# First sigmoid signals by itself, four places for survivals, and 84 of chunk 1's 124 convolution taps left to the feed-forward of chunk 0

## The chip, the cores and the metric

One core of a Trainium2 chip runs the whole program in one launch. The metric is device time in microseconds (us) of that launch, the median of several runs. Engines are named as in the profile: PE (TensorE, its matmuls), PEld (its weight loads), DVE (VectorE), ACT (ScalarE), POOL (GpSimd), SP (SyncE, which here issues every DMA). All arithmetic is 32-bit; a product of two numbers is made in three matmuls, from a high and a low part of each (the low part is a DVE subtraction behind an ACT copy).

## The reference, cut to what matters

One layer over 2048 prompt frames and 64 frames of a running stream, model width 1024:

```
h = RMSNorm(x);  a, gate, q, k, v = split(h @ w_in)
u = a * sigmoid(gate)
c = causal depthwise convolution of u, 31 taps, 512 channels
c = silu(LayerNorm(c)) @ w_pw
o[t] = sum over s < t of beta[t,s] * prod_{s<j<t} (1 - beta[t,j]) * v[s],   beta = sigmoid(q.k / 8)
x = x + concat(c, o) @ w_out
x = x + relu(RMSNorm(x) @ w_ff1)^2 @ w_ff2
```

The product over j is a running product from the right along each row of scores. The kernel makes it from sigmoid(-z), the "survivals" (tile `stay`), by a scan on DVE, and multiplies the result into sigmoid(z) (tile `beta`) on POOL.

## The kernel before

**Chunks and stages.** The prompt is cut into four chunks of 512 frames; the running stream goes with chunk 3. Each engine has its own instruction list, written out in one fixed order, and engines wait for each other on counted semaphores. The stages, in order: `ag(0)` and `kvq(0)` (chunk 0's projection and most of its convolution), `front` (92 slots: chunk 0's convolution end and attention, beside chunk 1's projection), `out(0)` (output projection and second norm of chunk 0), `window(0)` (128 slots of chunk 0's feed-forward, beside them chunk 1's last taps, LayerNorm, pointwise product and attention), `out(1)`, `ag(2)`, `kvq(2)`, `window(1)` with chunk 2's attention, `out(2)`, the same for chunk 3 with `window(2)`, and `window(3)` alone. One slot of a feed-forward window is twelve matmuls of 512 columns; 16 slots make one of 8 rounds (four slabs of w_ff1, then four of w_ff2).

**The convolution.** 124 taps (4 blocks of 128 channels, 31 each); a tap is one DVE instruction (line 1603) of 512 columns. `LATE[c]` is how many of chunk c's taps are left to the window; there they go two to a slot from slot 0 (`late_taps`). For chunk 1 the other taps are spread over the front by a list of due counts (`front_taps`). LayerNorm begins in slot `ln0(c) = (LATE[c] + 1) // 2` when the taps are done, the pointwise product 12 slots later, attention five slots after that (`att_first`) and up to slot 116 (58 in the front); the steps of attention are dealt out evenly over the slots in between.

**Attention.** One piece is 128 queries by up to 512 keys of one head. A step issues for several pieces at once, on each engine:

- PE: scores of piece z (line 2161, two PSUM banks), transposes of piece z-3 (2169, two banks), values of piece z-5 (2192)
- ACT (`att_sigmoids`): sigmoid(-z) into one of three `stay` tiles (1406), then sigmoid(z) into one of four `beta` tiles (1407), one signal `s_sg` behind both; then the high part of the transposed piece z-3 (1418)
- DVE (`att_parts`): for piece z-1 the edge copy (1810, pieces off the diagonal) and the scan (1811), both waiting for `s_sg`; then the low part of piece z-4 (1821); a mask (1799) on pieces of the diagonal
- POOL: `beta * stay` for piece z-1 (1135), waiting for the scan

ACT may overwrite a `stay` tile when the product that read it is done (`s_a`) and when the scan after it, which takes its first column over, is done (`s_scan`). PE may overwrite a bank of transposes when DVE has made the low part of the piece before last (`t_lo`).

**DMA.** Weights go through a ring of 8 slabs. At its first use a slab is loaded as 512 KB (line 734), split into high part (ACT, 1189) and low part (DVE, 1563) and stored (741, 1024 KB); later uses load both parts (736). All slabs of w_out and the feed-forward are first used in `out(0)` and `window(0)`. SP issues loads, stores, the keys (848), values (853) and queries (857) of attention and the mixed results (921, 936) in one order, sorted by planned ticks.

**Keys.** A block of 512 keys of the next head replaces the same block of the present one as soon as its last piece has been scored; with c+1 blocks in chunk c, its first use comes 2c+1 pieces later.

Of the kernel before, what the change touches and what calls it, by code (L numbers as in the profile page):

```python
# [5 lines left out]
F32 = mybir.dt.float32  # L6
F32R = mybir.dt.float32r
ALU = mybir.AluOpType
ACT = mybir.ActivationFunctionType
AX = mybir.AxisListType  # L10

P = 128
# [10 lines left out]
BANK = 512  # L23
# [10 lines left out]
KIB = 1024  # L34
# [24 lines left out]
def attention():  # L59

    out, z, m, v, o, hp = {}, 0, 0, 0, 0, 0
    for c in range(NC):
        for kind in range(2 if c == NC - 1 else 1):
            seq = []
            for head in range(NH):
                for p in range(1 if kind else 2):
                    for s in range(0 if kind else c, -1, -1):
                        rows = [(0, DEC)] if kind else [(P * i, P) for i in (2 * p, 2 * p + 1)]
                        for t, (q0, r) in enumerate(rows):
                            diag = kind == 1 or s == c  # L70
                            n = PAST + DEC if kind else q0 + P if diag else BANK
                            ends = t == len(rows) - 1
                            final = s == 0 and ends
                            brought = final and (kind == 0 or head == NH - 1)
                            seq.append(Piece(z, kind, head, p, t, q0, r, s * BANK, n, diag, ends, brought, m, v, o, hp, final))
                            z += 1
                            m += diag
                            v += ends
                    o += kind == 0 or head == NH - 1
                    hp += 1  # L80
            out[c, kind] = seq
    return out


ATT = attention()
# [39 lines left out]
LN_STEPS = 12  # L125

EARLY = 11
LATE = [20, 43, 36, 28]
FRONT = 92

MIX_AT = (62, 66, 71, 75)
# [3 lines left out]
def ln0(c):  # L135

    return (LATE[c] + 1) // 2

# [38 lines left out]
def gated_out(m):  # L177

    return max(8 * m + 8, ln0(0))
# [126 lines left out]
def build(nc, x_prompt, x_sample, cache_k, cache_v, state_conv, g_mix, w_in, w_dw, b_dw, g_cn, b_cn, w_pw,  # L306
# [3 lines left out]
    with ctx:  # L310
        top = [(nc.sbuf_base + 127) // 128 * 128]

        def region(size):
            o = top[0]
            top[0] += (size + 127) // 128 * 128
            return o

        def place(name, shape, dt=F32, offset=None):
            n = 4
            for s in shape[1:]:  # L320
                n *= s
            return nc.alloc_sbuf_tensor_at(name, shape, dt, offset=region(n) if offset is None else offset)
# [9 lines left out]
        o_cv = region(CB * CVP * 4)  # L332
        o_h = region(32 * KIB)
        o_a = region(56 * KIB)
# [34 lines left out]
        for c in range(2):  # L369
            n = TMAX if c else CHUNK  # L370
# [60 lines left out]
        aT_hi = place("aT_hi", [P, 2, 4, 2 * P], F32R, o_a + 22 * KIB)  # L431
        aT_lo = place("aT_lo", [P, 2, 4, 2 * P], F32R, o_a + 30 * KIB)
        beta = [place(f"beta{i}", [P, BANK], F32, o_a + (38 + 2 * i) * KIB) for i in range(4)]
        stay = [place(f"stay{i}", [P, BANK + 8], F32, o_a + 46 * KIB + i * (BANK + 8) * 4) for i in range(3)]
        o_o = o_a + 46 * KIB + 3 * (BANK + 8) * 4
        osb = place("osb", [P, 2 * P], F32, o_o)
        ohl = [place(f"ohl{i}", [P, 2, 2 * P], F32R, o) for i, o in enumerate((o_o + KIB, o_cv + 6 * KIB))]
# [22 lines left out]
        def sem(name):  # L460
            return ctx.enter_context(nc.semaphore(name))
# [29 lines left out]
        v_in = [sem(f"v_in{i}") for i in range(4)]  # L491
        q_in = [sem(f"q_in{i}") for i in range(3)]
        run_kq, run_v = sem("run_kq"), sem("run_v")
        z_ps, z_msk, s_sg, s_edge, s_scan, s_a, t_ps, t_hi, t_lo, v_ps, o_cp, o_sum, o_hi, o_lo = (
            sem(n) for n in ("z_ps", "z_msk", "s_sg", "s_edge", "s_scan", "s_a", "t_ps", "t_hi", "t_lo", "v_ps", "o_cp",
                             "o_sum", "o_hi", "o_lo"))
        o_st = [sem(f"o_st{i}") for i in range(2)]
        f1_ps, f_rel, f_sq, f_hi, f_lo, f2_ps, f2_add = (sem(n) for n in (
# [86 lines left out]
            return (before + e * (4 * len(splits(c)) + 2 * len(tiles(c))) + n) % 3  # L585

        Z_BANK, T_BANK, O_BANK = 3, 5, 7

        def ff_order(c):

# [42 lines left out]
        def front_taps():  # L633

            left, order, upto = [CW] * CB, [], []
            n, a = TAPS - LATE[1], gated_out(0)
            for t in range(FRONT):
# [13 lines left out]
        order_second, second_upto = front_taps()  # L651
        assert second_upto[-1] == TAPS - LATE[1]
        taps_in_order = [order_second if c == 1 else tap_order() for c in range(NC)]

        def taps_of(c, e):

            share = [3 if sec == "v" else 2 for sec, i, m in kvq_events(c)]
            rest, total = TAPS - 3 * EARLY - LATE[c], sum(share)
            return range(3 * EARLY + rest * sum(share[:e]) // total, 3 * EARLY + rest * sum(share[:e + 1]) // total)

        def late_taps(c, slot):
            return range(min(TAPS, TAPS - LATE[c] + 2 * slot), min(TAPS, TAPS - LATE[c] + 2 * slot + 2))

# [411 lines left out]
        def _(pool):  # L1075
# [51 lines left out]
            def att(c, step):  # L1127
                q = att_piece(c, step, 1)
                if q:
                    n = q.n - 1 if q.diag else q.n  # L1130
                    v = beta[q.z % 4]
                    pool.wait_ge(s_scan, q.z + 1)
                    if not q.diag:
                        pool.wait_ge(s_edge, q.z - q.m + 1)
                    nc.gpsimd.tensor_tensor(v[0:q.r, 0:n], v[0:q.r, 0:n], stay[q.z % 3][0:q.r, 1:n + 1],  # L1135
                                            ALU.mult).then_inc(s_a, 1)

            def window(c):
# [42 lines left out]
        def _(act):  # L1181
# [211 lines left out]
            def att_sigmoids(c, step):  # L1393
                q = att_piece(c, step, 0)
                if q is None:
                    return
                act.wait_ge(z_ps, q.z + 1)
                if q.diag:
                    act.wait_ge(z_msk, q.m + 1)
                if q.z >= 4:  # L1400
                    act.wait_ge(t_ps, q.z - 3)
                if q.z >= 3:
                    act.wait_ge(s_a, q.z - 2)
                    act.wait_ge(s_scan, q.z)
                z = ps[0:q.r, Z_BANK + q.z % 2, 0:q.n]
                nc.scalar.activation(stay[q.z % 3][0:q.r, 0:q.n], z, ACT.Sigmoid, scale=-1.0)  # L1406
                nc.scalar.activation(beta[q.z % 4][0:q.r, 0:q.n], z, ACT.Sigmoid).then_inc(s_sg, 1)  # L1407

            def att_later(c, step):
# [146 lines left out]
        def _(dve):  # L1556
# [244 lines left out]
            def att_parts(c, step):  # L1801
                q = att_piece(c, step, 1)
                if q:
                    v = stay[q.z % 3]
                    dve.wait_ge(s_sg, q.z + 1)
                    init = 1.0
                    if not q.diag:
                        dve.wait_ge(s_scan, q.z - 1)
                        init = stay[(q.z - 2) % 3][0:q.r, 0:1]
                        nc.vector.tensor_copy(v[0:q.r, q.n:q.n + 1], init).then_inc(s_edge, 1)  # L1810
                    nc.vector.tensor_tensor_scan(v[0:q.r, 0:q.n][:, ::-1], v[0:q.r, 0:q.n][:, ::-1],  # L1811
                                                 ones[0:q.r, 0:1].to_broadcast([q.r, q.n]), init,
                                                 ALU.mult, ALU.mult).then_inc(s_scan, 1)
                q = att_piece(c, step, TURN + 1)
                if q:
                    dve.wait_ge(t_hi, q.z + 1)
                    bank = ps[:, T_BANK + q.z % 2, :]
                    full = q.n // P
                    o = q.v % 2
                    if full:  # L1820
                        ins = nc.vector.tensor_tensor(aT_lo[:, o, 0:full, q.t * P:q.t * P + q.r],  # L1821
                                                      bank[:, 0:full * q.r].rearrange("p (a b) -> p a b", a=full),
                                                      aT_hi[:, o, 0:full, q.t * P:q.t * P + q.r].bitcast(F32), ALU.subtract)
                    if q.n % P:
                        w = q.n % P
                        ins = nc.vector.tensor_tensor(aT_lo[0:w, o, full, 0:q.r], bank[0:w, full * q.r:(full + 1) * q.r],
                                                      aT_hi[0:w, o, full, 0:q.r].bitcast(F32), ALU.subtract)
                    ins.then_inc(t_lo, 1)
                q = att_piece(c, step, VALUES + 2)
                if q and q.out:  # L1830
                    me = slice(0, P) if q.kind else slice(q.head % 2 * HD, q.head % 2 * HD + HD)
                    dve.wait_ge(o_hi, q.o + 1)
                    nc.vector.tensor_tensor(ohl[q.o % 2][me, 1, :], osb[me, :], ohl[q.o % 2][me, 0, :].bitcast(F32),
                                            ALU.subtract).then_inc(o_lo, 1)
                q = att_piece(c, step, VALUES + 1)
                if q and q.out:
                    dve.wait_ge(o_cp, q.o + 1)
                    for me, there, here in halves(q):
                        home = here(osb[me:me + HD, :])
                        ins = nc.vector.tensor_tensor(home, there(ps[me:me + HD, O_BANK, :]), home, ALU.add)  # L1840
                    ins.then_inc(o_sum, 1)
# [542 lines left out]
```

## Time and profile before

| | |
|---|---|
| median of 3 runs | 2859.02 us (2856.19 to 2863.88) |
| the profiled execution | 2860.11 us, span 2858.3 us |
| mean granted TensorE clock | 0.982 of full speed |
| PE busy | 2713.4 us, 95% of the span |
| DVE, ACT, POOL busy | 57%, 37%, 16% |
| DMA | 616 MB, mean 216 GB/s |

PE is busy nearly all the time from about 480 us on; its idle time lies mostly in the stages before (the front, out(0)) and in the attention of chunk 3. In time, `front` is about 170 to 410 us, `out(0)` 410 to 467, `window(0)` 467 to 911, the attention beside it 603 to about 880, `window(1)`'s attention about 1230 to 1550, `window(2)`'s 1940 to 2340.

### The profile page before, as it was taken

How to read it: one execution, taken by the hardware profiler on the slowest of the kernel's cores; microseconds unless marked ns; L12 is line 12 of the kernel's file. 1: busy time of each engine (PE TensorE's matmuls, PEld its weight loads, DVE VectorE, ACT ScalarE, POOL GpSimd, SP SyncE). 2: the span in 40 equal slices, each digit the busy share in tenths (PEclk: the TensorE clock that was granted, in tenths of full speed). 3: DMA queues.
4: the chain of work that ended last, by engine and by line, in shares of the span. 5: the costliest groups of instructions: out<-in, count | busy, mean ns of one | idle time of the engine just before them, and what ended most of it. 6: DMA issues, size and time to landing. Idle time of an engine off the chain costs nothing.

```text
span 2858.3 us, 37286 instructions
## 1 busy us (share of the span) xinstructions
PE 2713.4 (95%) x13872; PEld 2273.5 (80%) x13872; DVE 1640.4 (57%) x2653; ACT 1071.5 (37%) x2144; POOL 455.5 (16%) x460
## 2 busy tenths in 40 slices
PE   7878789999999999999999999999999999999999
PEld 6656577778888788778888797777788887898998
DVE  6887786757773468356665358636777742212122
ACT  4323533446562212345554112335666530221121
POOL 2212310012220011022221002102333310000000
PEclk9899899999999999999999999999999999999999
DMA  9596597777777658465554746844355457353442
GB/s 316 205 310 228 166 319 276 290 264 262 272 268 301 242 195 276 174 255 187 179 181 160 298 177 217 278 179 168 116 186 178 144 170 268 124 216 133 189 165 92
DMA packets 262046, 616.18 MB, mean 216 GB/s; under 512 B 23217, under 2 KB 159409, under 8 KB 213741
## 3 DMA queue, kind: packets, MB, share of 16 engines
q1 hardware_dynamic: 261869, 613.80, 60.0%
q8 instruction: 114, 1.87, 0.3%
q14 instruction: 63, 0.52, 0.0%
HBM read 444.79 MB, written 168.94 MB: 215 GB/s over the span
## 4 chain that ended last, share of the span: by engine, by line
PE 71%; DVE 14%; DMA 5%; ACT 4%; issue 4%; SPq 1%; POOL 1%; ACTq 0%; DVEq 0%; POOLq 0%
PE ps L1965 9%; PE ps L1967 9%; PE ps L1966 9%; PE ps L2221 7%; PE ps L2222 7%; PE ps L2223 7%; DVE stay L1811 4%; PE ps L2192 3%; PE ps L2169 3%; PE ps L2161 2%; DVE cacc L1603 2%; PE ps L2323 2%; PE ps L2324 2%; PE ps L2030 2%; PE ps L2325 2%
## 5 line engine op out<-in xcount | busy, mean ns | idle before, releaser
L1965 PE MATMUL ps<-h2T_hi,w_s 128*128 128x512 f32 (+1 forms) x1280 | 463.9, 362 | 7.6 <-DMA w_s<-w_scratch 3.4
L1135 POOL TENSOR_TENSOR beta<-beta,stay 128x512 f32<-128x512 f32 (+3 forms) x328 | 311.9, 951 | 918.9 <-DVE stay L1811 918.9
L1967 PE MATMUL ps<-h2T_hi,w_s 128*128 128x512 f32 (+1 forms) x1280 | 452.9, 354 | 0.0
L1966 PE MATMUL ps<-h2T_lo,w_s 128*128 128x512 f32 (+1 forms) x1280 | 452.5, 354 | 0.0
L1406 ACT ACTIVATE stay<-ps 128x512 f32<-128x512 f32 (+3 forms) x328 | 173.7, 529 | 427.0 <-DVE ps L1799 222.1
L1881 DVE TENSOR_TENSOR resid<-ps,resid 128x512 f32<-128x512 f32 x256 | 174.5, 687 | 246.3 <-PE ps L2223 245.9
L2221 PE MATMUL ps<-w_s,hid_hi 128*128 128x512 f32 x768 | 308.3, 401 | 0.0
L2223 PE MATMUL ps<-w_s,hid_hi 128*128 128x512 f32 x768 | 299.9, 390 | 0.0
L2222 PE MATMUL ps<-w_s,hid_lo 128*128 128x512 f32 x768 | 299.8, 390 | 0.0
L1481 ACT ACTIVATE ps<-ps 128x512 f32<-128x512 f32 (+1 forms) x160 | 81.8, 511 | 515.1 <-PE ps L1967 510.6
L1965 PEld LDWEIGHTS ps<-h2T_hi,w_s 128*128 128x128 f32 x1280 | 242.0, 189 | 39.1 <-DMA w_s<-w_scratch 3.6
L1967 PEld LDWEIGHTS ps<-h2T_hi,w_s 128*128 128x128 f32 x1280 | 241.8, 189 | 32.1
L1966 PEld LDWEIGHTS ps<-h2T_lo,w_s 128*128 128x128 f32 x1280 | 242.4, 189 | 27.9 <-issue 1.0
L1603 DVE SCALAR_TENSOR_TENSOR cacc<-uT,vecs,cacc 128x512 f32<-128x512 f32 (+1 forms) x360 | 259.8, 778 | 1.5
L1811 DVE TENSOR_TENSOR_SCAN stay<-stay,stay,ones 128x512 f32<-128x512 f32 x192 | 244.6, 1274 | 0.0
L1891 DVE TENSOR_TENSOR hid_lo<-ps,hid_hi 128x512 fp32r<-128x512 f32 x96 | 66.4, 691 | 259.4 <-ACT hid_hi L1491 259.4
L2169 PE MATMUL ps<-ident,beta 128*128 128x128 f32 (+1 forms) x1104 | 177.4, 276 | 28.6 <-DVE aT_lo L1821 27.8
L1821 DVE TENSOR_TENSOR aT_lo<-ps,aT_hi 128x512 fp32r<-128x512 f32 (+3 forms) x328 | 189.6, 578 | 14.9 <-ACT aT_hi L1418 9.7
L2161 PE MATMUL ps<-a_k,a_q 128*128 128x512 f32 (+3 forms) x640 | 183.4, 369 | 7.6 <-ACT beta L1407 4.5
L2169 PEld LDWEIGHTS ps<-ident,beta 128*128 128x128 f32 (+1 forms) x1104 | 132.9, 141 | 72.2 <-issue 47.4
L1418 ACT CAST aT_hi<-ps 128x512 fp32r<-128x512 f32 (+3 forms) x328 | 172.9, 527 | 21.3 <-PE ps L2169 16.8
L1407 ACT ACTIVATE beta<-ps 128x512 f32<-128x512 f32 (+3 forms) x328 | 172.1, 525 | 0.0
(211 smaller groups left out, 5212.2 us busy)
## 6 DMA issues: line engine op xcount, KB each, us to landing
w_s<-w_scratch SPq DMA_DIRECT2D x282, 1024.0 KB, 8.2
w_scratch<-w_s SPq DMA_DIRECT2D x94, 1024.0 KB, 8.7
w_raw<-in_w_ff SPq DMA_DIRECT2D x64, 512.0 KB, 5.5
a_k<-k_scratch SPq DMA_DIRECT2D x80, 256.0 KB, 3.8
a_v<-v_scratch SPq DMA_DIRECT2D x80, 256.0 KB, 3.9
a_q<-q_scratch SPq DMA_DIRECT2D x64, 256.0 KB, 4.5
w_raw<-in_w_in SPq DMA_DIRECT2D x20, 512.0 KB, 7.5
mix_scratch<-ohl SPq DMA_DIRECT2D x66, 128.0 KB, 3.0
```

The costliest lines, as they stand in the source:

```text
L1135: nc.gpsimd.tensor_tensor(v[0:q.r, 0:n], v[0:q.r, 0:n], stay[q.z % 3][0:q.r, 1:n + 1], ALU.mult).then_inc(s_a, 1)
L1603: nc.vector.scalar_tensor_tensor(out=acc, in0=uT[:, k, tap:tap + wd], scalar=vecs[:, k, tap:tap + 1], in1=acc, op0=ALU.mult, op1=ALU.add). ...
L1811: nc.vector.tensor_tensor_scan(v[0:q.r, 0:q.n][:, ::-1], v[0:q.r, 0:q.n][:, ::-1], ones[0:q.r, 0:1].to_broadcast([q.r, q.n]), init, ALU.mu ...
L1821: ins = nc.vector.tensor_tensor(aT_lo[:, o, 0:full, q.t * P:q.t * P + q.r], bank[:, 0:full * q.r].rearrange("p (a b) -> p a b", a=full), a ...
L1965: nc.tensor.matmul(out, w[0], x[0], start=start, stop=False)
L1966: nc.tensor.matmul(out, w[0], x[1], start=False, stop=False)
L1967: return nc.tensor.matmul(out, w[1], x[0], start=False, stop=stop)
L2161: ins = nc.tensor.matmul(ps[0:q.r, Z_BANK + q.z % 2, 0:q.n], x, a_k[:, k0:k0 + q.n], start=v == 0, stop=v == 1)
L2169: ins = nc.tensor.transpose(ps[0:w, T_BANK + q.z % 2, b * q.r:(b + 1) * q.r], beta[q.z % 4][0:q.r, b * P:b * P + w], ident[0:q.r, 0:q.r])
L2221: nc.tensor.matmul(o, hid_hi[x][:, k, q0:q0 + r], wh[:, c0:c0 + BANK], start=k == 0, stop=False)
L2222: nc.tensor.matmul(o, hid_lo[x][:, k, q0:q0 + r], wh[:, c0:c0 + BANK], start=False, stop=False)
L2223: ins = nc.tensor.matmul(o, hid_hi[x][:, k, q0:q0 + r], wl[:, c0:c0 + BANK], start=False, stop=k == 3)
```

## The change

Three edits. ACT's first sigmoid gets a semaphore `s_stay` of its own, and DVE's edge copy and scan wait for that in place of `s_sg`; POOL's product now waits for `s_sg` as well. From chunk 1 on (`OPENING` is the count of chunk 0's pieces, 32) there are four `stay` tiles instead of three, the fourth in the place of the convolution sums, and ACT's waits before the first sigmoid reach one piece further back. `LATE[1]` goes from 43 to 84: chunk 1's front takes 40 taps instead of 81, the late ones go on to slot 41 of window(0) instead of 21, `ln0(1)` moves from slot 22 to 42, the pointwise product from 34 to 54, the first attention step from 39 to 59; the last stays before slot 116.

```diff
-LATE = [20, 43, 36, 28]
+LATE = [20, 84, 36, 28]
...
-        stay = [place(f"stay{i}", [P, BANK + 8], F32, o_a + 46 * KIB + i * (BANK + 8) * 4) for i in range(3)]
+        stay = [place(f"stay{i}", [P, BANK + 8], F32, o) for i, o in enumerate(
+            [o_a + 46 * KIB + i * (BANK + 8) * 4 for i in range(3)] + [o_cv + 4032])]
...
+        OPENING = len(ATT[0, 0])
+
+        def stay_of(z):
+            return stay[z % 3] if z < OPENING else stay[z % 4]
...
                     v = beta[q.z % 4]
+                    pool.wait_ge(s_sg, q.z + 1)
                     pool.wait_ge(s_scan, q.z + 1)
...
-                    nc.gpsimd.tensor_tensor(v[0:q.r, 0:n], v[0:q.r, 0:n], stay[q.z % 3][0:q.r, 1:n + 1],
+                    nc.gpsimd.tensor_tensor(v[0:q.r, 0:n], v[0:q.r, 0:n], stay_of(q.z)[0:q.r, 1:n + 1],
                                             ALU.mult).then_inc(s_a, 1)
...
-                if q.z >= 3:
-                    act.wait_ge(s_a, q.z - 2)
-                    act.wait_ge(s_scan, q.z)
+                back = 3 if q.z < OPENING else 4
+                if q.z >= back:
+                    act.wait_ge(s_a, q.z - 2 if q.z < OPENING else max(q.z - 3, OPENING))
+                    act.wait_ge(s_scan, q.z + 3 - back)
                 z = ps[0:q.r, Z_BANK + q.z % 2, 0:q.n]
-                nc.scalar.activation(stay[q.z % 3][0:q.r, 0:q.n], z, ACT.Sigmoid, scale=-1.0)
+                nc.scalar.activation(stay_of(q.z)[0:q.r, 0:q.n], z, ACT.Sigmoid, scale=-1.0).then_inc(s_stay, 1)
                 nc.scalar.activation(beta[q.z % 4][0:q.r, 0:q.n], z, ACT.Sigmoid).then_inc(s_sg, 1)
...
-                    v = stay[q.z % 3]
-                    dve.wait_ge(s_sg, q.z + 1)
+                    v = stay_of(q.z)
+                    dve.wait_ge(s_stay, q.z + 1)
                     init = 1.0
                     if not q.diag:
                         dve.wait_ge(s_scan, q.z - 1)
-                        init = stay[(q.z - 2) % 3][0:q.r, 0:1]
+                        init = stay_of(q.z - 2)[0:q.r, 0:1]
```

## Rows read from the trace of the kernel before

**Rows 1.** The page: span, and busy time of each engine.

```profile
span 2858.3 us, 37286 instructions
...
PE 2713.4 (95%) x13872; PEld 2273.5 (80%) x13872; DVE 1640.4 (57%) x2653; ACT 1071.5 (37%) x2144; POOL 455.5 (16%) x460
```

**Rows 2.** Windows: stretch, length, busy per engine (PE, PEld, DVE, ACT, POOL), clock, DMA.

```profile
255.00:352.00 97.00, 72.67 (x364) 57.15 (x363) 68.79 (x140) 49.10 (x130) 32.80 (x35) 0.89 0.57 183
467.00:560.00 93.00, 91.21 (x378) 71.85 (x379) 69.26 (x96) 39.79 (x54) 2.69 (x3) 0.98 0.72 268
600.00:905.00 305.00, 302.19 (x1556) 254.57 (x1555) 211.71 (x327) 168.86 (x327) 58.99 (x64) 1.00 0.76 272
1230.00:1560.00 330.00, 328.74 (x1794) 279.33 (x1793) 224.43 (x375) 173.56 (x370) 92.97 (x94) 1.00 0.51 179
1935.00:2345.00 410.00, 392.04 (x2195) 327.40 (x2194) 294.84 (x512) 235.16 (x510) 133.11 (x136) 1.00 0.48 161
```

**Rows 3.** Waits of PE, 255 to 352 us: total us, times, longest.

```profile
PE ps L2169 <- DVE aT_lo L1821: 10.6, 13, 2.1
PE ps L2030 <- DVE raw_kq L1660: 9.0, 2, 5.1
```

**Rows 4.** Waits of DVE, the same stretch.

```profile
DVE stay L1811 <- ACT beta L1407: 19.8, 23, 1.2
```

**Rows 5.** Groups of ACT by line, the same stretch: busy us, mean ns.

```profile
L1407 ACT ACTIVATE beta<-ps 128x256 f32<-128x256 f32 (+3 forms) x31 | 13.6, 438 | 0.0
```

**Rows 6.** Instructions of line 1603, 365 to 422 and 467 to 532 us.

```profile
L1603 DVE SCALAR_TENSOR_TENSOR cacc_second<-uT,vecs,cacc_second x48: 742/745/752, 364.4 to 420.1; 128x512 f32<-128x512 f32 x48
...
L1603 DVE SCALAR_TENSOR_TENSOR cacc_second<-uT,vecs,cacc_second x42: 741/747/750, 467.0 to 531.5; 128x512 f32<-128x512 f32 x42
```

**Rows 7.** Waits of PE, 374 to 412 us.

```profile
PE ps L2042 <- DVE packed L1674: 4.4, 1, 4.4
```

**Rows 8.** Windows at the front's end, columns as in rows 2.

```profile
394.00:406.00 12.00, 8.87 (x26) 7.01 (x27) 10.27 (x17) 1.70 (x3) 2.87 (x2) 0.57 1.03 416
408.00:412.00 4.00, 2.56 (x15) 2.01 (x14) 3.62 (x7) 1.83 (x4) 2.06 (x1) 1.00 0.75 215
```

**Rows 9.** DMA queue, 374 to 452 us: packets, MB, share of 16 engines.

```profile
q1 hardware_dynamic: 20851, 26.97, 99.8%
```

**Rows 10.** Timeline of ACT and of PE, end of out(0).

```profile
451.88 1.06 ACT L1189 CAST w_s<-w_raw 128x1024 fp32r<-128x1024 f32 x1 [0.45 <-DMA w_raw<-in_w_ff]
...
467.18 0.79 PE L1965 MATMUL ps<-h2T_hi,w_s 128*128 128x512 f32 x1 [1.40 <-DVE h2T_lo L1588]
```

**Rows 11.** Line 848 (key loads), 600 to 900 us: who waited, landing.

```profile
  PE ps L2161: 2.5, 2
...
DMA to landing us min/median/max: 2.9/6.5/11.7
```

**Rows 12.** Instructions of line 2161 (scores), 600 to 900 us.

```profile
L2161 PE MATMUL ps<-a_k,a_q x128: 220/389/398, 602.9 to 857.2; 128*128 128x512 f32 x80, 128*128 128x128 f32 x16, 128*128 128x256 f32 x16, 128*128 128x384 f32 x16
```

**Rows 13.** Waits of PE, 1935 to 2345 us.

```profile
PE ps L2169 <- DVE aT_lo L1821: 15.8, 22, 1.2
```

**Rows 14.** Waits of DVE, 1935 to 2345 us.

```profile
DVE stay L1810 <- ACT beta L1407: 37.4, 64, 1.2
DVE stay L1811 <- ACT beta L1407: 27.2, 32, 1.2
```

**Rows 15.** Timeline of POOL and of DVE in chunk 3's attention.

```profile
2014.35 1.09 POOL L1135 TENSOR_TENSOR beta<-beta,stay 128x511 f32<-128x511 f32 x1 [2.34 <-DVE stay L1811]
...
2015.51 0.15 DVE L1810 COPY stay<-stay 128x1 f32<-128x1 f32 x1 [0.65 <-ACT beta L1407]
```

**Rows 16.** Timeline of DVE and of POOL in chunk 0's attention.

```profile
272.34 0.41 DVE L1833 TENSOR_TENSOR ohl<-osb,ohl 64x256 fp32r<-64x256 f32 x1
...
284.48 1.24 DVE L1833 TENSOR_TENSOR ohl<-osb,ohl 64x256 fp32r<-64x256 f32 x1
...
284.34 1.09 POOL L1135 TENSOR_TENSOR beta<-beta,stay 128x511 f32<-128x511 f32 x1 [1.34 <-DVE stay L1811]
```

More of the change, by code:

```diff
@@ L493, in build @@
         run_kq, run_v = sem("run_kq"), sem("run_v")
-        z_ps, z_msk, s_sg, s_edge, s_scan, s_a, t_ps, t_hi, t_lo, v_ps, o_cp, o_sum, o_hi, o_lo = (
-            sem(n) for n in ("z_ps", "z_msk", "s_sg", "s_edge", "s_scan", "s_a", "t_ps", "t_hi", "t_lo", "v_ps", "o_cp",
+        z_ps, z_msk, s_stay, s_sg, s_edge, s_scan, s_a, t_ps, t_hi, t_lo, v_ps, o_cp, o_sum, o_hi, o_lo = (
+            sem(n) for n in ("z_ps", "z_msk", "s_stay", "s_sg", "s_edge", "s_scan", "s_a", "t_ps", "t_hi", "t_lo", "v_ps", "o_cp",
                              "o_sum", "o_hi", "o_lo"))
```

## The prediction

> **What bounds the kernel now.** I read the page first, then a table of windows by stage, then PE's waits in the stages where it idles, then who makes those waits end, and last the DMA queue. PE is busy 2713.4 of 2858.3 us [rows 1], so whatever DVE, ACT or POOL save can return at most 145 us, and only where PE stands still. By stages [rows 2], it idles 24.3 us of 97 in chunk 0's attention, with a granted clock of 0.89, 1.8 of 93 beside the late taps of chunk 1, 2.8 of 305 in chunk 1's attention, 1.3 of 330 in chunk 2's and 18.0 of 410 in chunk 3's. The change can gain in the first and the last of these, and at the front's end, where PE stands before the transposes of line 2042 while DVE works through taps. It can lose in window(0), where PE hardly idles now.
>
> **Part 1: the first sigmoid's own signal.** In chunk 0's attention DVE stands 23 times, 19.8 us, for the second sigmoid [rows 4], though the scan reads only the first. The second is 438 ns on average [rows 5], so the scan can start that much sooner: 23 x 0.438 = 10.1 us from the chain of mask, sigmoid, scan, low part, mask. That is the upper end. The lower end is nothing, if the chain's other waits (a query load, the store of the mixed result, ACT's own copy behind the second sigmoid) end last. PE's two waits that hang on this chain are 10.6 and 9.0 us [rows 3], so there is room for all of it. I take half, 5 us.
>
> The added wait of POOL costs nothing: the scan, which POOL waits for anyway, starts behind the first sigmoid and lasts longer than the second. Behind POOL's waiting product stands only the next one. Should the scan ever end first, POOL would wait at most a second sigmoid's 0.44 us, for one piece.
>
> **Part 2: the four places, in chunk 3's attention.** PE's stall there is 15.8 us in 22 waits for the low part of line 1821 [rows 13]; DVE, which makes it, stands 64 + 32 times, 37.4 + 27.2 us, for the second sigmoid [rows 14]. With three places ACT can't begin piece z+1 before the scan of z has ended, so scan, two sigmoids and scan follow each other; with four and the early signal both sigmoids of z+1 lie beside the scan of z. Upper end: the whole 15.8 us and the 0.9 beside it.
>
> The lower end comes from POOL. In the steady pattern POOL's product begins at 2014.35 and lasts 1.09, to 2015.44; the edge copy before the next scan begins at 2015.51, having waited 0.65 us for the second sigmoid [rows 15]. A DVE instruction with two operands in SBUF seems to be unable to start beside such a product: line 1833 takes 0.41 us alone and 1.24 when it starts 0.14 us behind one, and it then ends 0.29 us behind the product's end [rows 16]. The scan too has two such operands. If it is held, it gains 0.07 us a piece off the diagonal and not 0.65, since the product is there until 2015.44. The 32 pieces of line 1811's own wait (the diagonal's, 27.2 us in all, 0.85 each) follow a mask and are further from the last product; they would keep their gain of up to 0.44 us, 14 us of chain in total. Also ACT no longer holds back the feed-forward's copy behind a first sigmoid that waits for a scan. Between all 16.7 and 5 (a third of the 14, as PE's stalls lie between the pieces that gain) I take 11 us: PE's stalls are 0.7 us each, about what a diagonal piece and the copy give back.
>
> The Trainium skill says this as a rule: "SBUF — State Buffer", section "SBUF: two separate sides", has DVE and GpSimd share one pair of ports under an exclusive lock, held for the whole instruction, also when the DVE instruction has two SBUF inputs; the other engine blocks fully. The trace agrees (1.24 against 0.41 us, rows 16). By that rule alone the early signal would be worth 0.07 us to each piece off the diagonal; it is weighed as the second rival below.
>
> In the attention of chunk 2 the same edit has 1.3 us of idle time to win; I count 1. It also shows that 105 steps in 81 slots, 1.3 a slot, need not make PE wait.
>
> **Part 3: 41 taps leave the front.** 48 taps of 745 ns run from 364 to 420 us [rows 6]; with 40 due instead of 81, the last 41 of them go, 30.5 us of DVE. For PE alone I count what stands around them: the wait of line 2042, 4.4 us [rows 7], the time lost at the lower clock behind it (8.87 us busy in 394 to 406 at a mean of 0.57 of 2.4 GHz, so largely at 1.2 GHz: 8.87 x 0.43 = 3.8), and 1.4 us idle at 408 to 412 [rows 8]: 9.6 us.
>
> But what comes next is a DMA. From 374 to 452 us the queue is 99.8% of 16 engines busy and moves 26.97 MB [rows 9], and SP issues in one order that the change leaves as it is. The last of the four feed-forward slabs makes ACT wait to 451.88, and DVE and ACT, in order, finish out(0)'s norm only behind these slabs; window(0) starts 15.3 us later, at 467.18 [rows 10]. So PE may reach the end of out(0) 9.6 us sooner and find the slabs no earlier. The gap that an earlier front closes in the queue is the 1 us in which its share is 0.75 [rows 8]; I allow as much again: 2 us. What part 1 gains comes ahead of this stretch and shifts it as a whole. Bounds: 0 and 9.6.
>
> **Part 4: the 41 taps in window(0), and what they push back.** They come at two a slot in slots 21 to 41. The stretch with such taps now has DVE busy 69 of 93 us and PE idle 1.8 [rows 2]; one more of the same costs 1 us, from 0 (all hidden behind twelve matmuls a slot) to 2. LayerNorm, pointwise product and their DMAs move 20 slots unchanged, into slots that look the same; the slabs of w_pw come one round later, before the same number of other slabs.
>
> Attention then has 57 slots for its 73 steps instead of 77. Work per PE is the same. What is shorter is the time in which keys must land: the next head's block is loaded three pieces before it is needed. 64 pieces are scored from 602.9 to 857.2 [rows 12], 4.04 us apart: three are 12.1 us. A bare slot is some 2.9 us (378 matmuls in 91.2 us [rows 2], times twelve), so the 77 slots' 77 x 4.04 x 73/77 = 295 us become 295 - 20 x 2.9 = 237 us, 3.25 us a step, 9.7 for three. Landing takes 2.9 to 11.7 us, median 6.5, SP's own delay comes on top, and two of 14 loads already make PE wait, 2.5 us [rows 11]. 2.4 us less for each: those two and perhaps a third wait longer or for the first time, 5 us. Bounds: 0 and 14 x 2.4 = 34. DVE's and ACT's load there rises from 212 and 169 of 305 us [rows 2] by a fifth to a quarter and stays under PE's.
>
> **Sum.** The profiled execution took 2860.1 us around a span of 2858.3: 2860.1 - 5 - 11 - 1 - 2 + 1 + 5 = 2847.1. It lies 1.1 above the median of the runs, 2859.0, so 2846 is forecast for the median, 0.45% faster.
>
> **Rivals.** *The DMA is not what ends out(0).* The queue's share counts packets that overlap; in 394 to 406 it moves 416 GB/s [rows 8], and at that rate 26.97 MB take 65 us, not 78. Then the 9.6 us of part 3 stand in full: 7.6 more, 2838. Against it: ACT waits for the last slab [rows 10]. The Trainium skill's "DMA: Bandwidth & Descriptors", section "Specifications", gives 435 GB/s as the fabric's ceiling, which by itself leaves that room; no run here shows the mean of 346 of this stretch rising.
>
> *POOL's product holds the scan*, so window(2) gives 3 us instead of 11, or the DMA eats the front's chain as well: 2854, within 0.3%. For it: rows 15 and 16. Against: stalls of 0.7 us are small beside 0.85 on the diagonal.
>
> *Slower: keys land late.* If each of the 14 loads of chunk 1's attention is as late as the shorter time makes it, 34 us instead of 5, the sum is 2860.1 + 15 = 2875, 2874 for the median. It decides from where the waits of line 2161 for `a_k` exceed 27 us in all. Against it: half of the loads land within 6.5 us [rows 11].
>
> **How the numbers follow.** 0.3% of the time, 8.6 us, is about what a measurement here can tell from no change. Forecast as summed 0.45 (2842 to 2851), no DMA bound 0.17, scan held or front lost 0.26, late keys 0.08, the other 0.04 on both sides. Faster by over 0.3% (under 2850.4): most of the forecast's case, all of the first rival, little of the second, 0.62; within: 0.29; slower: 0.09. The range must take in both the first and the second rival and an error of some 8 us beyond: 2830 to 2862.
>
> **What would show it.** Right: in chunk 0's and chunk 3's attention the waits of lines 1811 and 1810 for line 1407 are gone, and the wait of 2169 for 1821 in window(2) falls from 15.8 to about 5; no tap of chunk 1 after about 371 us, line 2042's wait gone, out(0) starting some 15 us sooner but window(0) only 7, with PE idle in front of line 1985 or 1965; `a_k` waits of some 7 us in window(0). The forecast is wrong if window(0) starts more than 12 us sooner, if scans in window(2) now start right at the end of POOL's products and PE's stall stays over 10, or if PE's waits in window(0) pass 20 us.

## The result: slower by 0.4%, the loss in one window

| | before | after |
|---|---|---|
| median of ten runs | 2860.4 us (2856.19 to 2863.88) | 2872.5 us (2865.57 to 2873.98) |
| ratio | | 1.0039, 95% interval 1.003 to 1.0049 |
| span of the profiled execution | 2858.3 us | 2870.4 us |

The change made the kernel slower by 12 us. 2846 was forecast, with a range up to 2862, so the result lies outside it and on the other side.

The stage boundaries, read in the timeline of PE (the first matmul of each stage), cut the 12.1 us of the two spans into four parts:

| stretch | before | after | change | forecast |
|---|---|---|---|---|
| start to window(0) | 467.2 | 467.5 | +0.3 | -7 |
| window(0), to out(1) | 453.1 | 478.6 | +25.5 | +6 |
| out(1) to window(2) | 876.7 | 877.1 | +0.4 | -1 |
| window(2) to the end | 1061.3 | 1047.2 | -14.1 | -11 |

Window(0) counts here to the first matmul of out(1): that is at 920.3 us in the kernel before, and its own last matmul starts at 919.0, not at about 911 as the section on the time before has it.

### The profile page after: what moved, and what is told of

Same layout as the page of the kernel before. It is cut to its first block and busy times, and to the rows that moved or that the text cites. A ratio compares the mean times of both kernels' runs of the same rounds, so it can differ in the third digit from the quotient of the medians.

```text
span 2870.4 us, 37421 instructions
## 1 busy us (share of the span) xinstructions
PE 2712.5 (94%) x13872; PEld 2274.2 (79%) x13872; DVE 1671.7 (58%) x2653; ACT 1069.2 (37%) x2144; POOL 449.2 (16%) x460
## 5 line engine op out<-in xcount | busy, mean ns | idle before, releaser
L1819 DVE TENSOR_TENSOR_SCAN stay<-stay,stay,ones 128x512 f32<-128x512 f32 x192 | 276.0, 1438 | 0.0
```

## The profile after

The page of the changed kernel, the span and the engines (lines are 7 or 8 higher than before in this kernel):

```profile
span 2870.4 us, 37421 instructions
...
PE 2712.5 (94%) x13872; PEld 2274.2 (79%) x13872; DVE 1671.7 (58%) x2653; ACT 1069.2 (37%) x2144; POOL 449.2 (16%) x460
```

PE does the same work in more time. DVE is busy 31 us longer with the same 2653 instructions, against [rows 1]: some of them now take longer; the run with a thin product below shows it for 20 us of them.

Windows over the stretches of [rows 2]: length, busy time of PE, PEld, DVE, ACT and POOL, clock, DMA.

```profile
255.00:352.00 97.00, 70.77 (x365) 56.57 (x363) 71.24 (x141) 48.27 (x128) 30.30 (x35) 0.91 0.58 185
467.00:560.00 93.00, 92.46 (x392) 75.14 (x393) 76.80 (x107) 29.19 (x40) 0.00 (x0) 0.97 0.67 255
600.00:905.00 305.00, 283.51 (x1434) 235.20 (x1434) 208.04 (x327) 163.44 (x320) 65.63 (x68) 0.98 0.68 235
...
1935.00:2345.00 410.00, 399.96 (x2249) 337.92 (x2248) 312.62 (x508) 234.19 (x507) 133.81 (x136) 1.00 0.48 159
```

The taps are hidden in 467 to 560 us, where PE idles 0.5 us. The loss is in the third row: in chunk 1's attention PE idles 21.5 us of 305 where it idled 2.8, and the clock is 0.98 in place of 1.00. As the stages have moved, here are the same columns for whole stretches, before and after: window(0), then window(2) up to out(3), with chunk 3's attention in it.

```profile
467.18:920.26 453.08, 446.36 (x2160) 368.94 (x2161) 299.98 (x447) 222.51 (x402) 62.46 (x68) 1.00 0.73 268
...
1797.00:2380.80 583.80, 560.41 (x2956) 463.49 (x2954) 365.65 (x633) 285.04 (x601) 143.97 (x145) 1.00 0.53 184
```

```profile
467.52:946.10 478.58, 456.10 (x2161) 373.14 (x2161) 326.89 (x488) 222.06 (x402) 65.63 (x68) 0.98 0.70 251
...
1823.20:2392.50 569.30, 557.00 (x2956) 464.29 (x2954) 384.06 (x633) 284.45 (x602) 144.74 (x145) 1.00 0.55 189
```

In window(0) PE idles 22.5 us in place of 6.7, and the same matmuls keep it busy 9.7 us longer, at a mean granted clock of 0.98 in place of 1.00: together the 25.5 us. The stretch with chunk 3's attention gained: 12.3 us idle in place of 23.4.

PE's waits in 600 to 905 us (total us, times, longest):

```profile
PE ps L2177 <- DVE aT_lo L1829: 8.7, 8, 2.5
PE ps L2169 <- DMA a_k<-k_scratch: 8.7, 3, 6.5
PE ps L2200 <- DMA a_v<-v_scratch: 1.6, 1, 1.6
```

Half of it is the late keys that the prediction looked for, with 8.7 us in place of some 7. The other half is the low part of the transposed product, of which it says nothing.

**What stands in front of the low part.** DVE's timeline ahead of one such wait, and PE's line that ends it:

```profile
754.23 4.63 DVE L1571 TENSOR_TENSOR w_s<-w_raw,w_s 128x1024 fp32r<-128x1024 f32 x4 [0.93 <-ACT w_s L1196]
758.77 0.95 DVE L1819 TENSOR_TENSOR_SCAN stay<-stay,ones 128x384 f32<-128x384 f32 x1
759.64 0.40 DVE L1829 TENSOR_TENSOR aT_lo<-ps,aT_hi 128x256 fp32r<-128x256 f32 x1
...
760.19 0.63 PE L2177 MATMUL ps<-ident,beta 128*128 128x128 f32 x4 [1.72 <-DVE aT_lo L1829]
```

Four new w_ff2 slabs of a round are due at once, and their low parts (the splitting of a weight at its first use) stand in DVE's list in one block of 4.63 us. The scan and the low part of attention come behind it, in order, and PE may not overwrite the bank before. DVE is far from full in this stretch (208 of 305 us); here it is the order of its list that makes PE wait.

**What stands in front of the keys.** SP's timeline, and the wait of PE that the key load ends:

```profile
765.00 3.35 SPq L747 DMA_DIRECT2D w_scratch<-w_s  x4
768.45 1.20 SPq L740 DMA_DIRECT2D w_raw<-in_w_ff  x1
769.70 3.67 SPq L854 DMA_DIRECT2D a_k<-k_scratch  x1
...
782.29 1.22 PE L2169 MATMUL ps<-a_k,a_q 128*128 128x512 f32 x2 [6.50 <-DMA a_k<-k_scratch]
```

The same four slabs are stored, 4 MB, ahead of a key load of 256 KB, with one slab load of 512 KB between them; the keys land 12.6 us after their issue. Around the 6.50 us gap, in 780 to 800 us, the mean granted clock is 0.83, between the two levels of 1.2 and 2.4 GHz; in the kernel before it is 1.00 in the same 20 us.

**The front.** out(0) started 9.2 us sooner (400.78 against 410.03) and ended 0.3 us later. ACT's timeline in out(0) (the first slab of w_out, and the four of the feed-forward that made it wait in [rows 10]), PE's wait near the start, and the start of window(0), which answers to the last line of [rows 10]:

```profile
414.01 1.04 ACT L1196 CAST w_s<-w_raw 128x1024 fp32r<-128x1024 f32 x1 [10.41 <-DMA w_raw<-in_w_out]
...
447.86 4.01 ACT L1196 CAST w_s<-w_raw 128x1024 fp32r<-128x1024 f32 x4
...
419.63 0.69 PE L2050 MATMUL ps<-ident,packed 128*128 128x128 f32 x2 [6.81 <-ACT kqT_late L1302]
...
467.52 0.79 PE L1973 MATMUL ps<-h2T_hi,w_s 128*128 128x512 f32 x1 [1.40 <-DVE h2T_lo L1596]
```

ACT now stands 10.41 us for slabs of w_out that have not landed, and PE 6.81 us behind a copy that comes after their split on ACT. The wait for taps turned into a wait for a transfer. For the feed-forward's slabs at 447.86 it no longer waits.

**Chunk 3's attention.** The waits of PE and of DVE there, against [rows 13, 14]:

```profile
PE ps L2177 <- DVE aT_lo L1829: 5.3, 11, 0.7
...
DVE stay L1819 <- ACT stay L1414: 17.2, 32, 0.7
...
DVE stay L1818 <- ACT stay L1414: 5.9, 7, 1.3
```

## The experiments

The times are medians of four to ten runs, with the kernel before run on the same chip; it stood at 2858.95 to 2860.87 us throughout. Lengths of stages are read as above; window(0) lasts 453.1 us before and 478.6 after, and from window(2) to the end it is 1061.3 and 1047.2 us.

### Which edit loses, which gains

**LATE alone.**

```diff
-LATE = [20, 43, 36, 28]
+LATE = [20, 84, 36, 28]
```

> The kernel before with LATE[1] = 84 alone, three places and the old signal. Theory A, crowding: window(0) loses its 25 us because chunk 1's attention has 57 slots in place of 77, whatever the signal does; then out(1) starts about 945 us, window(2) keeps the 15.8 us of waits for the low part that it had before, and the time is about 2872 + 14 = 2886 us. Theory B, the four places and the early signal themselves upset window(0), since ACT runs further ahead there: then out(1) starts about 920 us and the time is 2855 to 2862 us.

Measured: 2896.5 us, ratio 1.013 (1.0115 to 1.0146). Window(0) lasts 487.2 us, window(2) to the end 1061.3 as before. PE's waits in 600 to 905 us:

```profile
PE ps L2169 <- DVE aT_lo L1821: 18.2, 16, 2.6
PE ps L2161 <- DMA a_k<-k_scratch: 6.2, 3, 4.7
```

The time is 10 us above what theory A gave, and theory B falls. The loss is that of LATE, and without the other two edits it is 34 us: they save 8.6 us of it in window(0), where the wait for the low part is 18.2 us without them and 8.7 with them.

**Early signal and four places, LATE[1] = 43.**

```diff
-LATE = [20, 84, 36, 28]
+LATE = [20, 43, 36, 28]
```

> The changed kernel with LATE[1] back at 43: early signal and four places alone. Theory A, crowding: out(1) starts about 918 to 920 us as before, window(2) gives its 14 us, and the time is about 2846 us, faster than both kernels. Theory B, signal and places upset window(0): out(1) starts about 945 us and the time is about 2871 us.

Measured: 2844.2 us, ratio 0.9947 (0.9932 to 0.9962): faster than both kernels, by 16 and 28 us. Window(0) lasts 453.8 us.

**The attention squeezed, without the taps.** As the run before, and:

```diff
 def att_first(c):
-    return pw_slot(c) + pw_step(c) * CB + 1
+    return pw_slot(c) + pw_step(c) * CB + 1 + (20 if c == 1 else 0)
```

> LATE[1] = 43 with early signal and four places, but chunk 1's attention still begins in slot 59 of window(0): the 73 steps in 57 slots without the 41 taps there. Theory A, crowding: the loss comes back without the taps, out(1) about 945 us, 2868 to 2873 us. Theory C, the taps in slots 21 to 41 or what they delay are what costs: out(1) about 920 us, about 2846 us.

Measured: 2873.45 us, ratio 1.0046 (1.0031 to 1.006), window(0) 480.5 us. Theory C falls: the taps cost nothing in window(0), the later start of attention all of it.

**LATE[1] = 63.**

```diff
-LATE = [20, 84, 36, 28]
+LATE = [20, 63, 36, 28]
```

> The changed kernel with LATE[1] = 63: attention of chunk 1 in 67 slots of window(0), between 77 and 57. If the loss begins at once and is even, half of it is here, 12 to 14 us: about 2857 us. If the work on new slabs stays covered down to some density, under 6 us is lost: 2845 to 2850 us. In either case window(0) starts at 466 to 471 us, the front's taps being no bound.

Measured: 2870.7 us, ratio 1.004 (1.0025 to 1.0054), window(0) 481.6 us. Both expectations failed: with 67 slots the window is no shorter than with 57, so the number of slots isn't the measure. (Window(0) starts at 464.4 us, a little sooner than expected.) DVE's timeline ahead of PE's longest wait for a low part there, and that wait:

```profile
638.66 5.76 DVE L1571 TENSOR_TENSOR w_s<-w_raw,w_s 128x1024 fp32r<-128x1024 f32 x5
...
645.59 1.20 DVE L1571 TENSOR_TENSOR w_s<-w_raw,w_s 128x1024 fp32r<-128x1024 f32 x1
...
646.77 2.05 DVE L1819 TENSOR_TENSOR_SCAN stay<-stay,stay,ones 128x512 f32<-128x512 f32 x1
648.75 0.26 DVE L1829 TENSOR_TENSOR aT_lo<-ps,aT_hi 128x128 fp32r<-128x128 f32 x1
...
649.15 1.09 PE L2177 MATMUL ps<-ident,beta 128*128 128x128 f32 x4 [4.14 <-DVE aT_lo L1829]
```

Here five splits of slabs fall in one block ahead of a scan, a sixth behind it.

### Is it the work on new slabs?

**New slabs ready.** LATE[1] = 84; from round 2 of window(0) on no slab counts as new. They are read from the scratch, where another matrix lies.

```diff
-        if all((kind, j) != (k, i) for k, _, i in W[:n]):
+        if all((kind, j) != (k, i) for k, _, i in W[:n]) and not (kind in ("f1", "f2") and j >= 8):
...
-                    sp.dma_start(w_s[:, slot, :].bitcast(F32), w_d[W_ID[kind, j]]).then_inc(w_in_s[slot], 16)
+                    there = ("ag", j % 8) if kind in ("f1", "f2") and j >= 8 else (kind, j)
+                    sp.dma_start(w_s[:, slot, :].bitcast(F32), w_d[W_ID[there]]).then_inc(w_in_s[slot], 16)
```

> The changed kernel, LATE[1] = 84, without new feed-forward slabs from round 2 of window(0) on: these slabs are read as 1024 KB from places of the scratch that hold other weights, so no high or low part of them is made and none of them is stored (the feed-forward's weights are wrong for that). Theory A1, the work on new slabs (split on ACT and DVE, stores ahead of the keys) is what the denser attention no longer covers: window(0) takes 450 to 456 us in place of 478.6, PE's waits there for low parts and keys under 4 us, about 2848 us. Theory A2, 73 steps in 57 slots are too dense for the chain of attention by itself: window(0) still takes over 468 us, over 2862 us.

Measured: 2837.1 us, ratio 0.9919 (0.9903 to 0.9936). Window(0) lasts 455.1 us; out(1) to window(2) is 8.0 us shorter than in the changed kernel too, which puts the whole below the forecast; with thin stores, two runs below, it is 9.2 us shorter, so the stores seem to cost there as well. PE's waits in 600 to 905 us:

```profile
PE ps L2170 <- DMA a_k<-k_scratch: 5.2, 2, 3.1
PE ps L2178 <- DVE aT_lo L1830: 0.3, 1, 0.3
```

The 73 steps fit into 57 slots: the wait for the low part is gone, and 23.5 of the 25.5 us are back. Theory A2 falls, for all but 2.0 us. (Keys wait 5.2 us, over the 4 expected; each slab is now a load of 1024 KB in place of 512.)

**The same with LATE[1] = 63.**

> LATE[1] = 63 with early signal and four places, and without new feed-forward slabs from round 2 of window(0) on (read as 1024 KB from places that hold other weights, as in the run with slabs ready). With LATE[1] = 63 window(0) took 481.6 us, no less than with 84. If the work on new slabs is the cause there too, and where its bursts fall against the attention decides more than the number of slots, window(0) now takes 452 to 457 us and the time is 2835 to 2842 us. If something else in that order costs (two steps in one slot, the taps), window(0) stays over 468 us.

Measured: 2832.1 us, ratio 0.9915 (0.9896 to 0.9933); window(0) lasts 449.6 us in place of 481.6. So the new slabs are the cause with 67 slots as well; both numbers are a little below what was expected.

**Slabs split, but not stored.** LATE[1] = 84; the same slabs are loaded and split, 8 columns of each are stored. Later uses load other weights of the same size, as in the run with slabs ready; those lines are not shown.

```diff
-                sp.dma_start(w_d[W_ID[kind, j]], w_s[:, n % RING, :].bitcast(F32)).then_inc(w_st[n % RING], 16)
+                cols = 8 if kind in ("f1", "f2") and j >= 8 else 2 * SLAB
+                sp.dma_start(w_d[W_ID[kind, j]][:, 0:cols], w_s[:, n % RING, 0:cols].bitcast(F32)).then_inc(w_st[n % RING], 16)
```

> The changed kernel, LATE[1] = 84, with the new feed-forward slabs from round 2 of window(0) on still loaded and split, but of each only 8 columns stored (later uses read other weights). Under theory A1 this tells its two halves apart. If keys behind the stores on the DMA queue are the larger half, PE's wait for keys (8.7 us) goes and window(0) falls by 12 us or more, to 2860 us or less; if the split on DVE and ACT ahead of the scans is, only the keys' wait goes and window(0) falls by some 9 us at most, 2863 to 2867 us, with the wait for low parts still 8 us or more. Theory A2 (chain of attention alone): no change, 2870 us or more.

Measured: 2849.6 us, ratio 0.9966 (0.9955 to 0.9978), window(0) 468.2 us. The longest landing of a key load falls from 12.6 to 6.2 us, and PE's first wait in 600 to 905 us is now:

```profile
PE ps L2179 <- DVE aT_lo L1831: 12.9, 13, 2.5
```

No wait for keys is left. So of the 25.5 us the stores account for 10.4 (478.6 to 468.2), the splits for 13.1 (468.2 to 455.1), and 2.0 stay. This is the division with the stores taken away first; the other order was not tried, and the last step also doubles the size of these loads. The splits are work of ACT as well as of DVE, and no run takes DVE's alone away; PE's waits here, 12.9 us for DVE's low parts and 0.6 for ACT's sigmoids, point to DVE. The window fell by a little more than the 9 us that the second of the two expectations allowed, and by less than the first wanted; the total fell by more than either, as out(1) to window(2) was again shorter.

**The four slabs apart.** LATE[1] = 84; the w_ff2 slabs of window(0) are split and stored 1.5 ticks apart.

```diff
+def apart(n):
+    kind, c, j = W[n]
+    return 1.5 * (j % 4) if kind == "f2" and c == 0 else 0.0
...
-    return max(min(load_tick(n) + SPLIT_LAG, use_of(n)[0] - 2.0), -8.0)
+    return max(min(load_tick(n) + SPLIT_LAG + apart(n), use_of(n)[0] - 2.0), -8.0)
...
-    return max(min(load_tick(n) + SPLIT_LAG + 1.0, use_of(n)[0] - 1.5), split_tick(n))
+    return max(min(load_tick(n) + SPLIT_LAG + 1.0 + apart(n), use_of(n)[0] - 1.5), split_tick(n))
...
-                        if m < n and (load_tick(m) + STORE_LAG <= t or (n < len(W) and m == n - RING and load_tick(n) <= t)):
+                        if m < n and (load_tick(m) + STORE_LAG + apart(m) <= t or (n < len(W) and m == n - RING and load_tick(n) <= t)):
```

> The changed kernel, LATE[1] = 84, with the four w_ff2 slabs of a round split and stored 1.5 planned ticks apart in place of all at once. Theory A1, the bursts are what the shorter attention no longer covers (four low parts of 1.16 us in a row on DVE ahead of a scan, 4 MB of stores ahead of a key load): at least 10 of the 25 us in window(0) come back, 2862 us or less, and PE's waits there for the low part (8.7 us) and for keys (8.7 us) both fall by more than half. Theory A2, the chain of scores, sigmoid, scan and low part is itself too long for 1.3 steps a slot, or keys have too little lead wherever the stores stand: 2868 to 2874 us.

Measured: 2865.0 us, ratio 1.0018 (1.0008 to 1.0027), window(0) 474.7 us. PE's waits in 600 to 905 us:

```profile
PE ps L2182 <- DVE aT_lo L1834: 13.7, 7, 4.2
PE ps L2174 <- DMA a_k<-k_scratch: 3.7, 2, 2.2
```

This lies between the two expectations. Keys wait 5 us less, as A1 says, but low parts wait 5 us more: a split that stands alone can be reached by DVE before ACT has the slab's high part, and attention stands behind it then. DVE's line of one such split, and PE's wait behind it:

```profile
764.32 1.22 DVE L1576 TENSOR_TENSOR w_s<-w_raw,w_s 128x1024 fp32r<-128x1024 f32 x1 [2.91 <-ACT w_s L1201]
...
767.40 0.86 PE L2182 MATMUL ps<-ident,beta 128*128 128x128 f32 x3 [3.34 <-DVE aT_lo L1834]
```

Taken apart in this way, the burst still costs most of what it did.

### The front's end

**w_out not stored.** LATE[1] = 84, 8 columns stored of each w_out slab. Later uses load other weights of the same size; that line is not shown.

```diff
-                sp.dma_start(w_d[W_ID[kind, j]], w_s[:, n % RING, :].bitcast(F32)).then_inc(w_st[n % RING], 16)
+                cols = 8 if kind == "out" else 2 * SLAB
+                sp.dma_start(w_d[W_ID[kind, j]][:, 0:cols], w_s[:, n % RING, 0:cols].bitcast(F32)).then_inc(w_st[n % RING], 16)
```

> The changed kernel, LATE[1] = 84, with only 8 columns stored of each of the eight w_out slabs of out(0) (out(1) to out(3) read other weights of the same size): 8 MB less for the DMA between about 390 and 452 us. Theory D, the DMA queue sets the end of out(0): window(0) now starts at 455 to 460 us in place of 467.5, since PE was 9 us sooner at the start of out(0) already, and the time falls by 7 to 12 us. Theory E, the second norm's chain on DVE and ACT sets it: window(0) starts at 465 us or later and the time falls by under 3 us.

Measured: 2864.5 us, ratio 1.0012 (1.0001 to 1.0022), 8 us below the changed kernel. ACT's wait for the w_out slab and the start of window(0) are now:

```profile
406.01 1.05 ACT L1198 CAST w_s<-w_raw 128x1024 fp32r<-128x1024 f32 x1 [0.86 <-DMA w_raw<-in_w_out]
...
459.48 0.79 PE L1975 MATMUL ps<-h2T_hi,w_s 128*128 128x512 f32 x1 [1.40 <-DVE h2T_lo L1598]
```

With fewer bytes on the queue window(0) starts 8.0 us sooner, and the time falls by as much, so theory D holds. From ACT's first split of w_out to window(0) it is 53.5 us here and in the changed kernel. It agrees with all profiles taken: over six with LATE[1] = 43, out(0) starts at 409.1 us on average and window(0) at 466.8 (462.2 to 471.0); over five with 84 and all of w_out stored, at 400.8 and 466.6 (462.8 to 468.9). The 8.3 us that PE gains by fewer taps are gone 66 us later.

### The gain in chunk 3's attention

**Early signal alone**, LATE[1] = 43, three places everywhere (the fourth place and the change in ACT's wait for `s_a` go too):

```diff
-            return stay[z % 3] if z < OPENING else stay[z % 4]
+            return stay[z % 3]
...
-                back = 3 if q.z < OPENING else 4
+                back = 3
```

> LATE[1] = 43 and three places everywhere, the early signal alone. If the signal carries the gain from window(2) on (14 us), the time is 2844 to 2849 us. If the fourth place does (ACT can't begin before the scan has ended, whatever the signal says), the waits for the low part in window(2) stay over 12 us and the time is 2856 to 2860 us. With both needed for part of it, between these, some 5 to 8 us gained.

Measured: 2841.7 us, ratio 0.9935 (0.9917 to 0.9953), window(2) to the end 1048.0 us. DVE's waits for sigmoids and ACT's for scans, 1935 to 2345 us:

```profile
DVE stay L1819 <- ACT stay L1414: 17.2, 32, 0.7
DVE stay L1818 <- ACT stay L1414: 13.3, 44, 1.3
...
ACT stay L1414 <- DVE stay L1819: 47.6, 58, 1.5
```

**Four places alone**, LATE[1] = 43, the scan waiting for the second sigmoid (`s_stay` and POOL's wait for `s_sg` go too):

```diff
-                    dve.wait_ge(s_stay, q.z + 1)
+                    dve.wait_ge(s_sg, q.z + 1)
```

> LATE[1] = 43 and four places from chunk 1 on, the scan still waiting for the second sigmoid. If the fourth place carries the gain, DVE's waits for the second sigmoid are nearly gone without the early signal, and the time is 2844 to 2849 us; if the signal does, 2856 to 2860 us.

Measured: 2845.7 us, ratio 0.9946 (0.993 to 0.9962), window(2) to the end 1048.5 us. DVE's waits for sigmoids in the same stretch:

```profile
DVE stay L1818 <- ACT beta L1414: 27.3, 32, 1.2
...
DVE stay L1817 <- ACT beta L1414: 6.8, 8, 1.5
```

Each edit alone gives nearly the whole gain (1061.3 to 1048.0 and 1048.5; both together 1046.9), so neither is the single bearer that the expectations looked for. With four places alone DVE's waits for the second sigmoid, expected nearly gone, are still 34.1 us in place of 64.6 [rows 14]. With the signal alone ACT still stands 47.6 us for scans, but PE's wait for the low part in this stretch is 5.8 us, as short as with four places. The three versions with LATE[1] = 43 lie within their intervals of each other; the signal alone is the simplest.

**A thin product.** Signal and four places, LATE[1] = 43; in chunk 3 the product on POOL covers 8 columns.

```diff
+                    n = 8 if q.z >= att_end(NC - 2, "z") else n
                     nc.gpsimd.tensor_tensor(v[0:q.r, 0:n], v[0:q.r, 0:n], stay_of(q.z)[0:q.r, 1:n + 1],
```

> LATE[1] = 43, early signal and four places, with POOL's product in chunk 3's attention over 8 columns in place of up to 512 (beta of that chunk isn't multiplied). Theory P, POOL's product holds the scan that starts beside it: the scans there fall from a median of 1.42 us back to 1.27, some 15 us of DVE's time, and PE's remaining 5.5 us of waits for the low part fall to under 2: 2838 to 2841 us. Theory Q, the longer scans have another cause (ACT's or PE's traffic): median still over 1.38 us, 2842 to 2847 us.

Measured: 2837.8 us, ratio 0.9915 (0.9901 to 0.993). Groups of DVE by line, scans off the diagonal, 1935 to 2345 us (busy us, mean ns), in the kernel before, with the whole product and with the thin one:

```profile
L1811 DVE TENSOR_TENSOR_SCAN stay<-stay,stay,ones 128x512 f32<-128x512 f32 x96 | 122.3, 1274 | 0.0
```

```profile
L1819 DVE TENSOR_TENSOR_SCAN stay<-stay,stay,ones 128x512 f32<-128x512 f32 x96 | 142.8, 1488 | 0.0
```

```profile
L1820 DVE TENSOR_TENSOR_SCAN stay<-stay,stay,ones 128x512 f32<-128x512 f32 x96 | 122.2, 1274 | 0.0
```

Theory P holds: 20.6 us of DVE's time are scans that last longer beside a product. In the kernel before they were not held. The wait for the low part falls from 5.5 to 1.3 us, and window(2) to the end from 1046.9 to 1040.8: 6 us that the held scans cost now, at most: the thin product also ends sooner for what waits for it, and that was not tried apart.

## Why the prediction was wrong

**The step that failed is Part 4**, its sum for the attention of window(0): "two and perhaps a third wait longer or for the first time, 5 us", and the sentence that DVE's and ACT's load "stays under PE's". The term was +5; it measured +25.5 with the taps. The taps themselves were hidden, as forecast (+1 was allowed, the squeezed run shows none). For the keys the mechanism was right, three loads late as forecast, and the size off: 8.7 us and 1.6 of values in waits, 10.4 in the window's length. What was missing is 13.1 us of low parts behind the splits of new slabs. The load of an engine over 305 us was compared with PE's, and what its list puts in front of attention was left out.

The block of 4.6 us is not enough by itself. The kernel before has four such blocks in chunk 1's attention, 4.6 to 5.2 us from first to last, with 4.04 us from piece to piece [rows 12], and PE hardly waits for low parts there, in 600 to 905 us:

```profile
701.75 4.62 DVE L1563 TENSOR_TENSOR w_s<-w_raw,w_s 128x1024 fp32r<-128x1024 f32 x4
...
PE ps L2169 <- DVE aT_lo L1821: 0.2, 1, 0.2
```

Nor is the density: 73 steps in 57 slots without these blocks leave 0.3 us of this wait. It takes both. The prediction reckoned 3.25 us from piece to piece, and it came out at 3.71 (64 pieces from 654.6 to 888.2 us); 16 of the 57 slots carry two steps, six of 67, none of 77. Which of these makes a block cost, the mean distance, the slots with two steps or the place of the block among them, no run separates; that six such slots lose as much as 16 speaks for the place.

Chunk 2's attention, which served as proof that 1.3 steps a slot need not make PE wait, lies in a window without new slabs, and so could not show it.

**The slower rival** has the right place, sign and nearly the number (2874; its own terms, -5 - 11 - 1 - 2 + 1 + 34, give 2875 for the median and not 2874). But its deciding mark, over 27 us of waits for keys, was not met: 8.7. That it came so near is luck, as the low parts make up for keys that were less late. It was given too small a chance, 0.08, with only one mechanism priced for it. The prediction's own sign of being wrong, over 20 us of waits of PE in window(0), did come: PE idles 21.5 us in 600 to 905.

**Part 3** forecast that the taps' end gives back little, because the DMA bounds out(0): right, and the gain was 0 rather than 2. The place was another one than the prediction named. It is not the last feed-forward slab at 452 us that holds the chain but w_out's first slabs at 414: without their stores ACT has the first at 406.01, and window(0) starts 8.0 us sooner. The rival without a DMA bound falls.

**Part 1** forecast 5 us in chunk 0's attention. DVE's wait for sigmoids did change its partner and fell from 19.8 [rows 4] to 11.9 us, but PE's idle time there is 26.2 us, against 24.3 in [rows 2]: the wait for the low part fell from 10.6 [rows 3] to 9.2 us and a query load took 3.4 us in its place. It gained nothing, its own lower end. What it might have gained would probably have been lost in out(0), as the 8.3 us of the taps were; no run shows that.

**Part 2** forecast 11 us and measured 14.1, inside its bounds (5 to 16.7). PE's wait for the low part fell from 15.8 [rows 13] to 5.3 us. The reason given, that three places force the two sigmoids between two scans, was too strong: the signal alone gains as much. The rival of the held scan describes a thing that is there, but as a cost of at most 6 us that is left, not as one that takes the gain away. A scan and the product beside it in chunk 3's attention:

```profile
2059.57 1.10 POOL L1142 TENSOR_TENSOR beta<-beta,stay 128x512 f32<-128x512 f32 x1 [1.36 <-DVE stay L1819]
```

```profile
2059.99 1.76 DVE L1819 TENSOR_TENSOR_SCAN stay<-stay,stay,ones 128x512 f32<-128x512 f32 x1
```

The scan ends at 2061.75, 1.08 us after the product's end at 2060.67. By the rule that the prediction took from the Trainium skill's "SBUF — State Buffer", section "SBUF: two separate sides", the whole scan would stand behind the product; the trace agrees nearly, as all but 0.2 us of the scan's usual 1.27 come after it.

## What to carry to other kernels

Before work is packed closer beside a dense engine, look on each in-order list for the blocks that can stand in front of it, and on the DMA queue for the bursts ahead of its loads, and not at the sums of busy time alone. That a block is harmless now does not show that it stays so: blocks of the same length went with 0.2 us of waits for low parts in 77 slots and 8.7 in 57. A stage that seems to show that a density is harmless shows it only if the same blocks and bursts occur in it. Of a change with several edits, run each alone: here two gained 16 us together, each of them alone about as much, and the third lost 28.

## What was not expected of the hardware

An instruction of DVE that is held by POOL's product shows up in the records as a longer one, not as a later one: in chunk 3's attention the median of the scans off the diagonal is 1.418 us in the changed kernel and 1.275 with the thin product, the longest 2.00 and 1.28, with the same shapes throughout. And a key load of 256 KB takes 12.6 us to land behind stores of 4 MB, 6.2 at most where these are thin. It need not be stores: with the slabs ready, where loads of 1024 KB take the place of both, it is 11.9 at most.
